# Dense values projected token-major: the input-projection weights move over stationary token rows, and the values stage is gone

## The chip, the core and the metric

One Trainium2 chip, one core of it. The metric is device time in microseconds of one execution of the whole layer, batch 1, 2048 tokens, width 1024. All times are in microseconds (us) unless marked ns. Engines: PE is the matrix engine (TensorE; its weight loads are listed apart, as PEld), DVE the vector engine, ACT the scalar engine, POOL GpSimd; SP is the engine that here only issues DMAs.

## The reference, cut to what matters

A transformer layer with two groups of attention heads that share one input projection.

```python
h = rmsnorm(x, norm1_g) * (1 + sc1) + sh1
proj = h @ w_in                                   # (2048, 3280)
aq, ak, av, bq, bk, bv, iq, ik, iw = split_columns(proj)   # av: 512 columns
for each block of 128 queries:
    # group A: differential attention, 4 heads, two softmax maps per head
    attn = softmax(q1 @ k1.T * scale + bias) - lam * softmax(q2 @ k2.T * scale + bias)
    oa = rmsnorm(attn @ av[:q_end], subln_g) * (1 - lam_init)
    # group B: an indexer scores every key, top 256 keys per query, 8 heads share bk, bv
    score = sum_h iw[:, h] * relu(iq[:, h] @ ik.T)
    ob = softmax over the chosen keys of (q @ bk.T) @ bv
x = x + g1 * (concat(oa, ob) @ w_out)
x = x + g2 * (relu(h2 @ w_ff1) ** 2 @ w_ff2)
return rmsnorm(x, final_g)
```

`av`, the dense values, are the 512 projection columns this change is about. In `attn @ av` the matrix engine needs them with tokens on the partitions.

## The kernel before

Four stages follow one another. Every projection product is made of three matmuls, since each float32 operand is split into a high and a low part (hi·hi, hi·lo, lo·hi).

**Index projection** (`index_projection`) normalises and turns x into `ht_hi` and `ht_lo`: 1024 features on partitions (8 slices `k`), four groups `g` of 512 tokens. It projects the indexer's columns.

**Indexing** (`indexing`, some 765 us) does two things at once. The indexer's scores (L825 on PE, relu on ACT at L857, weighted add on DVE at L928) and, for blocks 2 to 11, a bisection for the top 256 (counts on ACT, judging on DVE). In between, as filler on PE, the 17 remaining column tiles of the input projection (`REST_TILES`, tiles 0 to 16 of 128 columns; 8 to 11 hold the dense values and are `FULL_TILES`). A tile has four units, one for each group of 512 tokens; a unit has eight steps, one for each `k`, of three matmuls (L843: 128 weight columns loaded, 512 tokens moving). Such a unit is evacuated by ACT (L883) and, for the low part, by DVE (L988), and stored to DRAM by POOL's queue, features on rows. A unit of a full tile has no low part (ACT L879, stored at L774 to `scr.av`, features on rows too).

The order on each engine is fixed at build time by `indexing_plan`: a greedy pass over streams of jobs with assumed costs. A projection step is assumed to cost 0.68 us on PE and comes after score jobs in priority. A unit's first step waits for the evacuation of the unit four before.

**Values** (`values`): loads `scr.av` group by group, turns it on PE (four transposes for 128 tokens, L1050), copies it to `va` with ACT (L1030); and turns the sparse group's values `bv` from its two parts by a product with an identity (L1052), copied to `vb` by DVE (L1036).

**Attention** (`attention`): order again from a plan. SP loads the query units and the keys, group of 512 by group; PE makes scores (L2582), DVE reads them with the bias table added (L2795), ACT takes exponentials, PE turns the probabilities (L2598) and multiplies by `va` (L2619) or `vb` (L2613). One tile `mixst` takes a group's output, and POOL's queue stores it (L2547); the next group's output waits for that store. POOL begins with resetting semaphores, two `iota`s (L2520, L2523) from which DVE builds the bias table, and a load of one saved score block (`rank_in`, L2531). Then `output_mlp`, bound by PE, follows.

Each stage's block of instructions ends with POOL waiting for all stores; the engines meet there.

## Time and profile before

| | us |
|---|---|
| time, median of 3 runs | 3682.78 |
| lowest and highest run | 3681.52, 3685.25 |
| span of the profiled execution | 3673.6 |
| PE busy, share of the span | 88% |
| indexing: first to last projection matmul | 356.8 to 1121.9 |
| values stage: first to last matmul | 1136 to 1163 |
| attention's first score | 1168.46 |

The three runs are not listed with the profiled execution's own time apart from them; its span is 9.2 us below their median, and that is what lies around the span. In the profile a matmul's duration (0.39 us at 512 columns) is longer than the distance to the next one, because they overlap. How fast PE runs is read from the distance between starts.

### The profile page before, as it was taken

What the parts mean: (1) busy time and instruction counts of PE and PEld (TensorE: products, weight loads), DVE (VectorE), ACT (ScalarE), POOL (GpSimd) and SP (SyncE); (2) the same over time, 40 slices, a digit from 0 to 9 for tenths busy, and PEclk for the clock granted to TensorE, in tenths of its full rate; (3) what the DMA queues carried; (4) which work ended last, traced back from release to release, by engine and by line L of the source; (5) the groups of instructions that cost most, each with busy time, mean ns of one, the idle gap of its engine ahead of it and who ended that gap; (6) DMA issues with size and microseconds to landing.
All of it is one profiled execution on the core that took longest, in us unless ns stands there. A gap on an engine that the chain in (4) does not pass through costs nothing. (4 is left out here: it accounts for less than half of the span.)

```text
span 3673.6 us, 44993 instructions
## 1 busy us (share of the span) xinstructions
PE 3250.9 (88%) x15808; PEld 2610.3 (71%) x15808; DVE 2538.3 (69%) x4800; ACT 1831.4 (50%) x3051; POOL 368.9 (10%) x587
## 2 busy tenths in 40 slices
PE   4986888899797798977789989889989999999999
PEld 3775666777685576755667768768868887888887
DVE  6542688877892677676776657788887875665676
ACT  3211677877673787878867643332232222322233
POOL 1010011110101100000000000012212220000131
PEclk8997999999896899999899999989999999999999
DMA  6354333322336432111111124644454445664565
GB/s 220 126 196 121 106 105 102 95 84 67 103 101 189 127 99 65 48 45 32 39 35 30 52 101 162 218 149 155 147 171 155 155 146 206 223 235 155 199 214 206
DMA packets 334617, 475.95 MB, mean 130 GB/s; under 512 B 29056, under 2 KB 218704, under 8 KB 333984
## 3 DMA queue, kind: packets, MB, share of 16 engines
q1 hardware_dynamic: 285936, 308.29, 26.6%
q0 software_dynamic: 48464, 164.88, 12.7%
q8 instruction: 123, 2.02, 0.2%
q14 instruction: 94, 0.77, 0.1%
HBM read 316.07 MB, written 156.98 MB: 129 GB/s over the span
## 5 line engine op out<-in xcount | busy, mean ns | idle before, releaser
L2099 PE MATMUL m_ps<-m_h,w_hi 128*128 128x512 f32 x1792 | 560.7, 395 | 43.1 <-DVE m_h L1728 21.0
L2099 PEld LDWEIGHTS m_ps<-m_h,w_hi 128*128 128x128 f32 x1792 | 340.9, 191 | 117.7 <-DVE m_h L1728 30.0
L928 DVE SCALAR_TENSOR_TENSOR rank<-spare,iw,rank 128x1024 f32<-128x1024 f32 (+5 forms) x330 | 332.1, 1021 | 69.7 <-ACT spare L857 64.5
L2116 PE MATMUL m_ps<-w_hi,a_hi 128*128 128x512 f32 x896 | 350.7, 391 | 12.0 <-DVE w_lo L1936 8.9
L2099 PE MATMUL m_ps<-m_h,w_lo 128*128 128x512 f32 x896 | 352.7, 394 | 0.0
L2116 PE MATMUL m_ps<-w_lo,a_hi 128*128 128x512 f32 x896 | 350.2, 391 | 0.0
L2116 PE MATMUL m_ps<-w_hi,a_lo 128*128 128x512 f32 x896 | 350.1, 391 | 0.0
L857 ACT ACTIVATE spare<-isps 128x1024 f32<-128x1024 f32 (+5 forms) x352 | 279.7, 812 | 114.5 <-PE isps L825 80.7
L825 PE MATMUL isps<-ki,iq_hi 128*128 128x512 f32 (+3 forms) x608 | 238.8, 394 | 88.9 <-ACT spare L857 68.7
L2659 ACT ACTIVATE pt<-tps 128x512 f32<-128x512 f32 (+1 forms) x432 | 233.3, 573 | 109.6 <-PE tps L2598 53.1
L2598 PE MATMUL tps<-ident,probs 128*128 128x128 f32 x1632 | 238.7, 287 | 46.0 <-DVE probs L2814 28.7
L2598 PEld LDWEIGHTS tps<-ident,probs 128*128 128x128 f32 x1632 | 190.1, 146 | 97.8 <-DVE probs L2814 36.7
L2795 DVE CUSTOM_DVE_ANT_0 probs<-sps,bias 128x1024 f32<-128x1024 f32 (+7 forms) x176 | 165.8, 962 | 124.2 <-PE tps L2598 70.8
L2647 ACT ACTIVATE probs<-probs,stat 128x128 f32<-128x128 f32 (+15 forms) x192 | 231.1, 1204 | 34.5 <-DVE stat L2804 34.2
L864 ACT ACTIVATE below<-rank,tk 128x640 int8<-128x640 f32 (+9 forms) x210 | 228.6, 1090 | 39.1 <-DVE tk L957 35.9
L1516 ACT ACTIVATE a_hi<-a_lo 128x2048 fp32r<-128x2048 f32 x56 | 107.3, 1916 | 271.5 <-DMA a_lo<-dram_aop 271.5
L825 PE MATMUL isps<-ki,iq_lo 128*128 128x512 f32 (+3 forms) x608 | 228.7, 385 | 0.0
L843 PE MATMUL r_ps<-ht_hi,r_w_hi 128*128 128x512 f32 x544 | 219.5, 404 | 8.8 <-DVE r_ev_lo L988 5.7
L1933 DVE TENSOR_TENSOR a_lo<-a_lo,a_hi 128x2048 fp32r<-128x2048 f32 x56 | 141.2, 2521 | 117.9 <-ACT a_hi L1516 117.7
L825 PEld LDWEIGHTS isps<-ki,iq_hi 128*128 128x128 f32 x608 | 120.3, 198 | 140.5 <-ACT spare L857 54.1
L843 PE MATMUL r_ps<-ht_lo,r_w_hi 128*128 128x512 f32 x544 | 217.2, 399 | 0.0
L843 PE MATMUL r_ps<-ht_hi,r_w_lo 128*128 128x512 f32 x544 | 215.9, 397 | 0.0
(285 smaller groups left out, 7032.8 us busy)
## 6 DMA issues: line engine op xcount, KB each, us to landing
w_raw<-in_w_ff SPq DMA_DIRECT2D x136, 512.0 KB, 5.3
dram_aop<-a_out POOLq DMA_DIRECT2D x224, 256.0 KB, 2.6
a_lo<-dram_aop SPq DMA_DIRECT2D x56, 1024.0 KB, 5.3
ada_w<-in_w_ada POOLq DMA_DIRECT2D x16, 1024.0 KB, 6.6
q_hi<-dram_proj_hi SPq DMA_DIRECT2D x128, 128.0 KB, 3.0
q_lo<-dram_proj_lo SPq DMA_DIRECT2D x128, 128.0 KB, 3.0
iq_hi<-dram_proj_hi SPq DMA_DIRECT2D x224, 64.0 KB, 2.4
iq_lo<-dram_proj_lo SPq DMA_DIRECT2D x224, 64.0 KB, 2.5
```

The source lines that it names most:

```text
L825: mm = nc.tensor.matmul(sps[:, job.n % 2, a:b], q[:, job.unit % IQU, job.head % 2, :], ki[:, job.c * SCH + a:job.c * SCH + b], start=part ...
L843: mm = nc.tensor.matmul(ps[:, job.n % 4, :], a[:, i % 2, job.part, :], b[:, job.g, job.part, :], start=job.part == 0 and m == 0, stop=job. ...
L857: nc.scalar.activation(spare[:, job.n % 2, 0:job.width], sps[:, job.n % 2, 0:job.width], ACT.Relu).then_inc(s_relu, 1)
L864: nc.scalar.activation(below[:, q, 0:length].bitcast(I8), ranks[job.k % 3][:, 0:length], ACT.Sign, bias=tk[:, q, TK_NT:TK_NT + 1], accum_o ...
L928: nc.vector.scalar_tensor_tensor(out=dst, in0=got, scalar=w, in1=dst, op0=ALU.mult, op1=ALU.add).then_inc(s_acc, 1)
L1933: nc.vector.tensor_tensor(s_lo[:, c % RING], s_lo[:, c % RING].bitcast(F32), s_hi[:, c % RING].bitcast(F32), ALU.subtract).then_inc(c_sl, 1)
L2099: mm = nc.tensor.matmul(ps[:, b], w[:, m % WOPS, k, :], hop[:, j, h, :, k, :], start=fresh and k == 0 and i == 0, stop=k == KH - 1 and i == 2,
L2116: mm = nc.tensor.matmul(ps[:, t], a[:, c % RING, k, t * P:(t + 1) * P], w[:, c % RING, k, :], start=first and i == 0, stop=last and i == 2 ...
L2598: tr = nc.tensor.transpose(tps[:, job.turn % TR, (2 * kk + hh) * P:(2 * kk + hh + 1) * P], probs[:, g.heads[hh] % 4, (job.first + kk) * P: ...
L2647: nc.scalar.activation(row, row, ACT.Exp, bias=stat[:, job.hm % 8, 2:3], scale=slope, accum_out=stat[:, job.hm % 8, 3:4]).then_inc(s_exp, 1)
L2659: nc.scalar.activation(pt[:, job.slot % PT, 0:width], tps[:, job.of.turn % TR, 0:width], ACT.Copy).then_inc(s_te, 1)
L2795: nc.vector.tensor_tensor_reduce(out=row[:, job.c * SCH:job.c * SCH + job.width], in0=sps[:, job.score.n % 2, 0:job.width], in1=add, scale ...
```

## The change

1. The full tiles come last in `REST_TILES`, after all tiles that have a low part.
2. For them operands change places: the token rows `ht` are loaded as the stationary operand (128 tokens), and 128 weight columns move over them. A step has 12 matmuls of 128 columns in place of 3 of 512; a unit 96 in place of 24. The plan's assumed costs are the same as before.
3. The unit's result then has tokens on partitions; it is stored token-major, `scr.av` being `[SEQ, 512]`, 128 partitions by 4 pieces of 512 bytes.
4. `values` is gone. POOL's queue loads `va` straight from `scr.av` in four pieces of 1024 KB: the first after the two iotas, the others after the first three stores of attention outputs. PE waits for a piece where it first uses it.
5. `bv` is loaded whole in attention and turned there by 32 small matmuls between the first and the second score; DVE copies `vb` once.
6. The waits for the last stores of indexing move from the end of its block into attention's POOL stream (`last_stores`, `s_settled`). SP loads the first keys piece by piece with a semaphore each (`s_first`), query units 1 and 2 between them.

```diff
-        self.av = t("av", [A_HEADS * 2 * DH, SEQ])
+        self.av = t("av", [SEQ, A_HEADS * 2 * DH])
...
-REST_TILES = list(range(INDEX_TILES[0]))
 FULL_TILES = range(R_AV // P, R_AV // P + 4)
+REST_TILES = [tile for tile in range(INDEX_TILES[0]) if tile not in FULL_TILES] + list(FULL_TILES)
...
-                        pool.dma_start(scr.av[row:row + P, job.g * GT:(job.g + 1) * GT],
-                                       ev_hi[:, job.n % 2, :].bitcast(F32)).then_inc(s_st[job.n % 2], 16)
+                        tok = slice(job.g * GT, (job.g + 1) * GT)
+                        pool.dma_start(scr.av[tok, row:row + P].rearrange("(t p) e -> p t e", p=P),
+                                       ev_hi[:, job.n % 2, :].bitcast(F32).rearrange("p (t e) -> p t e", e=P)
+                                       ).then_inc(s_st[job.n % 2], 16)
...
-                for n in range(2):
-                    pool.wait_ge(s_st[n], 16 * stored[n])
-                    pool.wait_ge(s_mst[n], 16 * ((SPLIT - 2) // 2))
-                for n in range(3):
-                    pool.wait_ge(s_kept[n], 16 * kept[n])
+                last_stores.extend([(s_st[n], 16 * stored[n]) for n in range(2)])
...
+                        if job.tile in FULL_TILES:
+                            t = job.part * WT // KT
+                            tok = slice(t * P, (t + 1) * P)
+                            steps_of = KT * WT // KT
+                            for k in range(job.part * steps_of % KT, job.part * steps_of % KT + steps_of):
+                                for m, (a, b) in enumerate(((ht_hi, w_hi), (ht_lo, w_hi), (ht_hi, w_lo))):
+                                    mm = nc.tensor.matmul(ps[:, job.n % 4, tok], a[:, job.g, k, tok], b[:, i % 2, k, :],
+                                                          start=k == 0 and m == 0, stop=k == KT - 1 and m == 2,
+                                                          skip_group_check=True)
...
-def values(nc, keep, scr, late, block, va, vb):
...
             load_unit(0)
-            for dst, row in places:
-                load_keys(dst, row, 0)
+            for n in range(A_HEADS):
+                load_keys(*places[n], 0, s_first[n])
+            for part, src in enumerate((scr.proj_hi, scr.proj_lo)):
+                sp.dma_start(bv[:, part].bitcast(F32), src[R_BV:R_BV + DH, :]).then_inc(s_bv, 16)
+            load_unit(1)
...
+            for signal, count in last_stores:
+                pool.wait_ge(signal, count)
+            pool.sem_inc(s_settled, 1)
+
+            def load_values(g):
+                pool.dma_start(va[:, g * TG:(g + 1) * TG, :],
+                               scr.av[g * GT:(g + 1) * GT, :].rearrange("(n p) e -> p n e", p=P)).then_inc(s_va[g], 16)
+
+            load_values(0)
...
                     outs += 1
+                    if outs < NG:
+                        load_values(outs)
...
+                    if job.n == 1:
+                        pe.wait_ge(s_idv, 1)
+                        pe.wait_ge(s_bv, 32)
+                        for kt in range(NB):
+                            for part in range(2):
+                                mm = nc.tensor.matmul(sps[:, 1, kt * DH:(kt + 1) * DH],
+                                                      bv[:, part, kt * P:(kt + 1) * P], ident_r[:],
+                                                      start=part == 0, stop=part == 1)
+                        mm.then_inc(s_vt, 1)
+                        pe.wait_ge(s_vb, 1)
...
+                        if kt // TG == valued:
+                            pe.wait_ge(s_va[valued], 16)
+                            valued += 1
```

The names in the rows below: `isps` are the indexer's score sums, `r_ps` the sums of the projection tiles, `sps` attention's scores. A row says output, the moving operand, the loaded operand, and the output's shape.

PE at the end of indexing, before: the last score job, and the first of the 84 projection matmuls that follow it.

```order
L825 MATMUL isps<-ki,iq_hi 128x512
L825 MATMUL isps<-ki,iq_lo 128x512
L843 MATMUL r_ps<-ht_hi,r_w_hi 128x512
L843 MATMUL r_ps<-ht_lo,r_w_hi 128x512
L843 MATMUL r_ps<-ht_hi,r_w_lo 128x512
```

The same place in the changed kernel.

```order
L827 MATMUL isps<-ki,iq_hi 128x512
L827 MATMUL isps<-ki,iq_lo 128x512
L850 MATMUL r_ps<-r_w_hi,ht_hi 128x128
L850 MATMUL r_ps<-r_w_hi,ht_lo 128x128
L850 MATMUL r_ps<-r_w_lo,ht_hi 128x128
```

After the last score now stand 660 matmuls of 128 columns (55 steps) where 84 of 512 (28 steps) stood; 876 of 128 columns stand between scores, from score matmul 788 of 1216 on.

PE where attention begins, before.

```order
L1050 MATMUL v_psum<-ident,av_t 128x128 x4
L1052 MATMUL w_psum<-ident_v,bv_t 128x64 x2
L2559 UNCONDITIONAL_BRANCH
L2582 MATMUL sps<-ka,q_hi 128x128
L2582 MATMUL sps<-ka,q_lo 128x128
```

And in the changed kernel.

```order
L850 MATMUL r_ps<-r_w_lo,ht_hi 128x128
L739 UNCONDITIONAL_BRANCH
L2542 UNCONDITIONAL_BRANCH
L2578 MATMUL sps<-ka,q_hi 128x128
L2578 MATMUL sps<-ka,q_lo 128x128
L2562 MATMUL sps<-ident_v,bv_t 128x64 x32
L2578 MATMUL sps<-ka,q_hi 128x128
L2578 MATMUL sps<-ka,q_lo 128x128
```

The values stage's 96 instructions are gone, and 32 of them stand behind the first score. POOL's queue at the start of attention, before:

```order
L2520 IOTA second 128x2048
L2523 IOTA probs 128x128
L2531 DMA rank_in<-dram_ranks 128x1664
L2547 DMA dram_mix<-mixst 128x256 x2
L2547 DMA dram_mix<-mixst 128x128 x4
```

And in the changed kernel.

```order
L2490 IOTA second 128x2048
L2493 IOTA probs 128x128
L2500 DMA va<-dram_av 128x4x512
L2505 ISA
L2512 DMA rank_in<-dram_ranks 128x1664
L2528 DMA dram_mix<-mixst 128x256
L2500 DMA va<-dram_av 128x4x512
L2528 DMA dram_mix<-mixst 128x256
L2500 DMA va<-dram_av 128x4x512
L2528 DMA dram_mix<-mixst 128x128
L2500 DMA va<-dram_av 128x4x512
```

A load of values now stands ahead of each of the second, third and fourth output store.

## Rows read from the trace of the kernel before

**Rows 1.** The page: span, and the slices' granted clock in tenths

```profile
span 3673.6 us, 44993 instructions
...
PEclk8997999999896899999899999989999999999999
```

**Rows 2.** Busy time of the engines by stretch; then clock, DMA share, GB/s

```profile
core 0: us, PE busy (x) PEld busy (x) DVE busy (x) ACT busy (x) POOL busy (x), PEclk, DMA share, GB/s
356.00:934.00 578.00, 499.65 (x2108) 396.71 (x2109) 452.53 (x1031) 430.43 (x716) 64.66 (x110) 0.94 0.31 93
934.00:970.00 36.00, 21.60 (x95) 17.04 (x94) 31.08 (x47) 22.92 (x31) 2.70 (x5) 0.86 0.17 54
970.00:1103.00 133.00, 129.83 (x565) 104.09 (x566) 117.58 (x109) 95.72 (x106) 14.96 (x26) 0.97 0.35 114
1122.30:1169.00 46.70, 26.40 (x99) 20.01 (x99) 6.12 (x21) 12.15 (x21) 3.60 (x5) 0.55 0.80 213
```

**Rows 3.** The same stretches, projection matmuls (L843) alone: PE, PEld

```profile
356.00:934.00 578.00, 340.61 (x1320) 249.45 (x1320) 0.94 0.31 93
970.00:1103.00 133.00, 50.45 (x181) 33.68 (x182) 0.97 0.35 114
1103.00:1122.30 19.30, 19.24 (x84) 15.45 (x83) 1.00 0.36 136
```

**Rows 4.** The same stretch, score matmuls (L825) alone: PE, PEld

```profile
356.00:934.00 578.00, 208.33 (x788) 151.41 (x789) 0.94 0.31 93
```

**Rows 5.** Timeline, weight loads around two pairs of 128-column matmuls: start, duration

```profile
435.38 0.19 PEld L825 LDWEIGHTS isps<-ki,iq_lo 128*128 128x128 f32 x1
435.49 0.19 PEld L825 LDWEIGHTS isps<-ki,iq_hi 128*128 128x128 f32 x1
435.60 0.19 PEld L825 LDWEIGHTS isps<-ki,iq_lo 128*128 128x128 f32 x1
```

**Rows 6.** Timeline, the matmuls there

```profile
435.38 0.22 PE L825 MATMUL isps<-ki,iq_hi 128*128 128x128 f32 x1
435.44 0.27 PE L825 MATMUL isps<-ki,iq_lo 128*128 128x128 f32 x1
435.55 0.45 PE L825 MATMUL isps<-ki,iq_hi 128*128 128x512 f32 x1
```

**Rows 7.** Timeline, weight loads in attention, clock full, merged runs

```profile
1300.29 1.07 PEld L2598 LDWEIGHTS tps<-ident,probs 128*128 128x128 f32 x10 [0.79 <-DVE probs L2814]
...
1302.12 2.31 PEld L2619 LDWEIGHTS ops<-va,pt 128*128 128x128 f32 x20
```

**Rows 8.** Timeline, the end of indexing on ACT and POOL

```profile
1122.28 0.69 ACT L883 ACTIVATE r_ev_hi<-r_ps,r_scale 128x512 fp32r<-128x512 f32 x1 [4.80 <-PE r_ps L843]
1124.58 0.54 POOL L780 DMA_DIRECT2D dram_proj_lo<-r_ev_lo  x1
1128.85 1.83 POOL L2520 IOTA second<- 128x2048 int32 x1 [3.73 <-DMA dram_proj_lo<-r_ev_lo]
```

**Rows 9.** Timeline, SP's queue: values' first load, and attention's loads

```profile
1128.09 0.40 SPq L1021 DMA_DIRECT2D av_t<-dram_av  x1
...
1150.50 1.26 SPq L2485 DMA_DIRECT2D q_hi<-dram_proj_hi  x2
1151.80 1.27 SPq L2485 DMA_DIRECT2D q_lo<-dram_proj_lo  x2
1153.12 0.61 SPq L2494 DMA_DIRECT2D ka<-dram_proj_hi  x1
1153.78 0.60 SPq L2494 DMA_DIRECT2D ka<-dram_proj_lo  x1
```

**Rows 10.** Timeline, PE: the values stage (one of 16 rounds), the first two scores

```profile
1137.52 1.12 PE L1050 MATMUL v_psum<-ident,av_t 128*128 128x128 f32 x4
1138.57 0.63 PE L1052 MATMUL w_psum<-ident_v,bv_t 64*128 64x64 f32 x2
1139.13 1.11 PE L1050 MATMUL v_psum<-ident,av_t 128*128 128x128 f32 x4
...
1168.46 0.45 PE L2582 MATMUL sps<-ka,q_hi 128*128 128x128 f32 x1 [5.29 <-DMA kb<-dram_proj_lo]
...
1168.92 0.41 PE L2582 MATMUL sps<-ka,q_hi 128*128 128x128 f32 x1
```

**Rows 11.** DMAs from 1120 to 1200: count, KB each, median us to landing

```profile
av_t<-dram_av SPq DMA_DIRECT2D x4, 1024.0 KB, 5.7
dram_mix<-mixst POOLq DMA_DIRECT2D x4, 64.0 KB, 2.4
```

**Rows 12.** Low-part evacuations on DVE (L988): min/median/max ns

```profile
L988 DVE SCALAR_TENSOR_TENSOR r_ev_lo<-r_ps,r_scale,r_ev_hi x52: 741/746/752, 373.0 to 1123.0; 128x512 fp32r<-128x512 f32 x52
```

More of the change, by code:

```diff
@@ L1058 @@
+    return last_stores
 P_A11, P_S2, P_A12, P_S1, P_S3, P_S4, P_A22 = range(7)
@@ L2449, in attention @@
         ops = ctx.enter_context(nc.psum_tensor("ops2", [P, 2 * P], F32))
-        s_k = [sem(f"s_k_in{n}") for n in range(NG)]
+        s_first = [sem(f"s_first_k_in{n}") for n in range(2 * A_HEADS + 1)]
+        s_k = [sem(f"s_k_in{n}") for n in range(1, NG)]
+        s_va = [sem(f"s_va_in{n}") for n in range(NG)]
+        s_bv = sem("s_bv_in")
+        s_idv = sem("s_ident_v")
+        s_settled = sem("s_last_stores_over")
+        s_vt = sem("s_bv_turned")
+        s_vb = sem("s_vb")
         s_q = [sem(f"s_q_in{n}") for n in range(QU)]
@@ L2494, in load_keys @@
                     sp.dma_start(dst[r * DH:(r + 1) * DH, keys].bitcast(F32),
-                                 src[row:row + DH, keys]).then_inc(s_k[g], 16)
+                                 src[row:row + DH, keys]).then_inc(signal, 16)
             def load_chosen(b):
@@ L2499, in load_chosen @@
                     sp.wait_ge(s_bias, b - 2)
+                if b == 3:
+                    sp.wait_ge(s_settled, 1)
                 sp.dma_start(chosen[:, 0:P * (b + 1)], scr.masks[b, :, 0:P * (b + 1)]).then_inc(s_ch, 16)
             load_unit(0)
-            for dst, row in places:
-                load_keys(dst, row, 0)
+            for n in range(A_HEADS):
[3 more added lines that the diff above has]
+            load_unit(1)
+            for n in range(A_HEADS, 2 * A_HEADS):
+                load_keys(*places[n], 0, s_first[n])
+            load_unit(2)
+            load_keys(*places[-1], 0, s_first[-1])
             load_chosen(2)
-            pieces = [(dst, row, g) for g in range(1, NG) for dst, row in places]
-            for n in range(1, len(units)):
+            pieces = [(dst, row, g, s_k[g - 1]) for g in range(1, NG) for dst, row in places]
+            for n in range(QU, len(units)):
                 load_unit(n)
-                if n <= len(pieces):
-                    load_keys(*pieces[n - 1])
+                if n - QU < len(pieces):
+                    load_keys(*pieces[n - QU])
                 b = units[n][1]
@@ L2574, in _ @@
                         pe.wait_ge(s_sf, before.read)
+                    if job.n == 1:
[8 more added lines that the diff above has]
+                        pe.wait_ge(s_vb, 1)
+                    place = 2 * A_HEADS if job.what == "sparse" else 2 * job.head + (job.what == "map2")
+                    if place not in first_places:
+                        first_places.add(place)
+                        pe.wait_ge(s_first[place], 32)
                     keys = kb if job.what == "sparse" else ka[:, 2 * job.head + (job.what == "map2"), :]
@@ L2638, in _ @@
         def _(act):
+            nc.scalar.activation(ident_r[:], keep.ident[0:DH, 0:DH], ACT.Copy).then_inc(s_idv, 1)
             for half in range(2):
@@ L2864, in hybrid_block @@
                 vb = inner.enter_context(nc.sbuf_tensor("vb", [P, NB, DH], F32))
-                s_va, s_vb = values(nc, keep, scr, late, block, va, vb)
-                done = attention(nc, keep, scr, late, block, va, vb, s_va, s_vb, spent)
+                done = attention(nc, keep, scr, late, block, va, vb, last_stores, spent)
             output_mlp(nc, keep, scr, late, block, done, x, subln_g, w_out, w_ff1, w_ff2, final_g, out)
```

102 lines of the change are left out of this document (31 added, 71 removed).

## The prediction

> **What bounds the kernel now.** I went from the page to the stretches, and from there to the single instructions. The page says that PE is what nearly the whole span is made of, at a clock mostly full [rows 1], so a change that adds PE work has to find idle PE time or cost its length. The table of stretches cuts the part that is touched. From 356 to 934 indexing has PE 86% busy and DVE 78%, neither full [rows 2]: scores, relus and adds wait for one another. From 970 to 1103 PE is 98% busy [rows 2]. From 1103 to 1122.3 there is nothing left but 84 projection matmuls in 19.3 us, with PE full [rows 3]: 0.229 us each, which is the distance between two of 512 columns at the full clock (2.4 GHz). I take 0.228. Then comes a stretch of 46.7 us in which PE has 26.4 us of small work at a clock of 0.55 [rows 2]: the meeting of the engines, the values stage, the first loads of attention.
>
> So in the first half the touched work hides partly, in the second half not at all.
>
> **The change part by part.**
>
> *The price of one 128-column matmul with its own load.* The trace before has this very shape: scores of 640 keys end in a hi and a lo matmul of 128 columns. The first to second start is 0.06 us apart, what 128 columns take; but the second to the next is 0.11 [rows 6], because the loads stand 0.11 apart, 435.38, 435.49, 435.60 [rows 5]. A 512-column matmul hides such a load, a 128-column one does not: the stream runs at the pace of the loads. Long runs at full clock say the same: 10 loads in 1.07 us, 0.107 each, and 20 in 2.31, 0.1155 or less each [rows 7]. I take 0.11, with 0.107 and 0.115 as ends.
>
> The 16 full units have 384 matmuls at 0.228, 87.6 us, before, and 1536 at 0.11, 169.0 us, after: **81.4 us more PE work** in the indexing stage for the same product. The evacuations (ACT 0.6 to 0.7 us each) and stores are as many as before and have ten microseconds a unit; they are hidden. The token-major stores have more and shorter pieces, and also have that time.
>
> The Trainium skill, "TensorE: Matmul & The Clock Gate", section "Back-to-back issue gap", gives 81 ns for a stream of loads and 128-column matmuls, and 131 ns at 512 columns. The rows above contradict the second (0.229) and stand above the first (0.11). By its 81 ns the 1536 would take 124 us, 37 more than before; the sum below does not use it.
>
> *Where it stands.* The plan that fixes the order still assumes 0.68 us for a step, and a step is now 12 × 0.11 = 1.32 us. And by moving tiles with a low part forward it delays steps behind DVE's evacuations, so fewer steps find a place between scores: 55 steps (660 matmuls) stand behind the last score where 28 (84) stood. I add up in three pieces, counting in the order and pricing scores at 0.228 (512 columns), 0.168 (384) and 0.114 (256, 128).
>
> (a) Up to score matmul 788, at 934 us in the trace [rows 4]. Before, 1320 projection matmuls stand ahead of it [rows 3]; after, 1248: 72 fewer, 16.4 us less PE work. But 52 units with a low part are done by then in place of 39 (1320/24 = 55 units less the 16 full), 13 × 0.746 us [rows 12] = 9.7 us more on DVE. With both engines waiting for each other in this stretch I take 0, with ends −16 (PE decides) and +10 (DVE decides).
>
> (b) From score 788 to 1216, 934 to 1103 us, 169 us. Before: 228 projection matmuls 52.0 + 428 score matmuls 90.6 = 142.6 of PE work, so 26 us of real gaps, some 16 of them before 970 (PE busy 21.6 of 36 there [rows 2]). After: 90.6 + 876 × 0.11 = 96.4, together 187.0. The added 44 us fill gaps first: I leave 7 of the 16 and 4 of the other 10, since more filler ahead of a score makes PE the one that is waited for. 187 + 11 = 198, **+29**. Ends: no gap left, +18; all gaps left, +44.
>
> (c) Behind the last score: 660 × 0.11 = 72.6 against 19.3, **+53**. Nothing else is there to hide it: DVE and ACT have no work left but evacuations. Ends 51 (at 0.107) and 57 (at 0.115).
>
> Indexing: 0 + 29 + 53 = **+82**.
>
> *The values stage.* Count from ACT's last evacuation, 1122.28 [rows 8]. Before, the second score begins at 1168.92 [rows 10], 46.6 later: both stores to land (SP goes on at 1128.09 [rows 9]), then 1 MB and 16 rounds of 1.61 us on a cold PE [rows 10], then keys and queries, of which the first score waits for the last one (5.29 us, kb [rows 10]). After: ACT 0.7, POOL's issue by +1.9, SP begins at about +2.1, since nobody waits for landing. Four query loads take 2.6 us of its queue, eight key loads 0.64 each, 5.1 [rows 9]; the two loads of bv 1.2: issued at +11. They are 512 KB each; with a landing somewhat under the 5.7 us of 1 MB [rows 11], +16. The 32 matmuls: a round of 1.61 less the four transposes' 1.12 is 0.49 for two [rows 10], 16 × 0.49 = 7.8 us cold (3.5 if the clock were full): +24. DVE's copy of 1024 columns some 1 us: the second score at +25. Gain 46.6 − 25 = **−22**. POOL's iotas (2.1 us, from +2) and DVE's table stood beside the values stage and are now in front of the first read, but end by +6, before the first score can be there (+9): nothing. Ends: −30 (fast landing, warm clock) and −14 (DMA slow while the queue is full).
>
> *Attention's start.* The loads of the pieces 1 to 3 of va (1 MB, 5.7 us [rows 11]) each go onto POOL's queue ahead of an output store that takes 2.4 us alone [rows 11], and the single `mixst` makes the next group wait for it. Groups come every 4 to 5 us there, so a store meets only the last microseconds of a load: 1 to 2 us three times, +4 (ends 0 and 12). Queries of units 1 and 2 come earlier, −1. **+3**. The rest of attention and the MLP have the same order and move as a whole.
>
> Sum: 82 − 22 + 3 = +63. Against the median, since the 9 us around the span stay: 3682.8 + 63 = **3746 us**, slower by 1.7%.
>
> **The rivals.**
>
> *The column pace decides (not slower).* If in a long row of these matmuls the loads ran under the matmuls completely, one would cost 0.057, half of 0.114 for 256 columns. Then (a) gives up to −8, (b) 876 × 0.057 = 50 against 52, −2, (c) 38 against 19, +18; with −22 and +3 it is −11: **3672**. For it speaks only that first distance of 0.06 [rows 6]; against it the loads' own distances [rows 5, 7]. It decides where the pace falls under about 0.066.
>
> *Halfway.* If the load is half hidden, 0.083 each: (c) 54.8, +35.5; (b) 90.6 + 72.7 = 163 with 14 us of gaps, +8; (a) 0; with −19: **3707**. The Trainium skill's 81 ns of that section ("TensorE: Matmul & The Clock Gate", "Back-to-back issue gap") is this case.
>
> *The gaps take it.* The stage has 119 us of gaps before 934. If the earlier placing lets PE run ahead, (a) is −16 and (b) +18: 55 − 22 + 3: **3719**. Against it: those gaps are waits for DVE and ACT, and the order is fixed.
>
> *Starved scores.* Each step ahead of a score now delays relu and add by 0.6 us more; where DVE, at 88% from 970 to 1103 [rows 2], then misses its turn, gaps add to gaps: (a) +10, (b) +44, (c) +57, less 19: **3775**, up to 3790.
>
> *The handover does not get shorter.* bv's load, 32 cold matmuls and the copy in a row, plus va's loads on the queue: gain 8 in place of 19: **3757**.
>
> **How the numbers follow.** Forecast 60% (its own range 3725 to 3770), column pace 6%, halfway 8%, gaps 10%, starved 9%, handover 7%. The likeliest is 3746. The range 3705 to 3785 takes in all but the column pace and the far end of starvation. A measurement can tell 0.2%, 7.4 us, from no change. Faster is the column pace alone, 6%; within 0.2% the space between it and halfway, 3%; slower the rest, 91%.
>
> **What would show it.** The 128-column matmuls at 0.107 to 0.115 us from start to start, loads at the same distance; the first of them 930 to 940 us into the span; the last score near 1132; 73 us of nothing but L850 behind it, and indexing's last matmul near 1204; the second score 25 us later, in place of 47; attention and MLP as long as before. I am wrong if L850's starts stand under 0.09 apart, if the last score comes before 1115 or after 1150, or if the first blocks of attention wait for va or for stores by more than 12 us.

## The result, and the profile after

The changed kernel takes 3759.07 us in the median of 4 runs (3751.91 to 3761.83), the kernel before on the same chip 3682.15 us (4 runs, 3676.18 to 3685.25). The ratio is 1.0202, with a 95% interval from 1.0186 to 1.0217: 76.9 us slower. The forecast was 3746, its range 3705 to 3785.

The profiled execution of the changed kernel has a span of 3750.0 us against 3673.6 [rows 1], so 76.4 us more: the two executions show nearly the whole difference of the medians. The changed kernel's profiled execution took 3751.91 us, so 1.9 us lie around its span and not the 9.2 named ahead of the prediction; it is 7 us under its median, and by the same 1.9 us so is that of the kernel before (an estimate, 3675.5), so the difference between the two stays. The page's span, and the granted clock in tenths, slice by slice:

```profile
span 3750.0 us, 47131 instructions
...
PEclk9997999989999699998889999989999999999999
```

The clock is as full as it was; time went somewhere else. The same stretches as in [rows 2], cut at the same events (score matmul 788, the last score, ACT's last evacuation, the second attention score). The columns are busy time and count of PE, PEld, DVE, ACT and POOL, then clock, DMA share and GB/s:

```profile
356.00:933.40 577.40, 488.37 (x2035) 386.09 (x2035) 461.80 (x1053) 434.01 (x718) 71.45 (x123) 0.92 0.32 98
933.40:1133.20 199.80, 193.77 (x1306) 177.06 (x1305) 140.21 (x137) 113.67 (x131) 13.57 (x20) 0.98 0.24 75
1133.20:1207.10 73.90, 73.90 (x662) 73.81 (x660) 2.04 (x2) 4.62 (x7) 5.06 (x7) 1.00 0.11 37
1207.10:1239.30 32.20, 7.76 (x36) 7.40 (x35) 3.54 (x8) 3.03 (x7) 4.13 (x5) 0.55 0.91 224
```

The first stretch is as long as before, the second has grown from 169 to 199.8 us and the third from 19.3 to 73.9. In the third the clock is full and PE never idle. The fourth has shrunk. Of the projection in token order alone (L850), PE, PEld, clock, DMA share, GB/s:

```profile
933.40:1133.20 199.80, 104.11 (x876) 104.82 (x877) 0.98 0.24 75
1133.20:1207.10 73.90, 73.71 (x660) 73.81 (x660) 1.00 0.11 37
```

660 of them stand behind the last score, and 73.9 us for 660 is **0.112 us each**. In that stretch the weight loads are as busy as the matmuls: 73.81 of 73.9 us. The timeline at 1150 us, first the matmuls and then the weight loads, start and duration:

```profile
1150.08 0.27 PE L850 MATMUL r_ps<-r_w_hi,ht_hi 128*128 128x128 f32 x1
1150.19 0.28 PE L850 MATMUL r_ps<-r_w_hi,ht_lo 128*128 128x128 f32 x1
1150.31 0.28 PE L850 MATMUL r_ps<-r_w_lo,ht_hi 128*128 128x128 f32 x1
```

```profile
1150.14 0.19 PEld L850 LDWEIGHTS r_ps<-r_w_hi,ht_lo 128*128 128x128 f32 x1
1150.25 0.19 PEld L850 LDWEIGHTS r_ps<-r_w_lo,ht_hi 128*128 128x128 f32 x1
1150.36 0.19 PEld L850 LDWEIGHTS r_ps<-r_w_hi,ht_hi 128*128 128x128 f32 x1
```

Matmuls and loads both stand 0.11 apart. This is the distance that the pair of short matmuls in the kernel before had shown [rows 5, 6].

The handover, on PE (the brackets give the idle time ahead and what ended it), and on SP's queue:

```profile
1215.12 0.44 PE L2578 MATMUL sps<-ka,q_hi 128*128 128x128 f32 x1 [7.92 <-DMA ka<-dram_proj_lo]
1230.97 7.01 PE L2562 MATMUL sps<-ident_v,bv_t 64*128 64x64 f32 x32 [15.20 <-DMA bv_t<-dram_proj_lo]
1239.30 0.47 PE L2578 MATMUL sps<-ka,q_hi 128*128 128x128 f32 x1 [1.32 <-DVE vb L2783]
```

```profile
1216.43 0.61 SPq L2471 DMA_DIRECT2D bv_t<-dram_proj_hi  x1
1217.09 0.60 SPq L2471 DMA_DIRECT2D bv_t<-dram_proj_lo  x1
```

ACT's last evacuation starts at 1207.23 and the second score at 1239.30, 32.1 us later, where it was 46.6 [rows 8, 10]. Of these 32, PE sits 15.2 waiting for `bv_t`, issued at 1216.4 and 1217.1 and there at 1230.97.

### The profile page after: what moved, and what is told of

It is laid out like the page before. It is cut to its first block and busy times, and to the rows that moved or that the text cites. A ratio compares the mean times of both kernels' runs of the same rounds, so it can differ in the third digit from the quotient of the medians.

```text
span 3750.0 us, 47131 instructions
## 1 busy us (share of the span) xinstructions
PE 3317.9 (88%) x16896; PEld 2700.3 (72%) x16896; DVE 2533.5 (68%) x4785; ACT 1822.4 (49%) x3035; POOL 378.4 (10%) x591
## 5 line engine op out<-in xcount | busy, mean ns | idle before, releaser
L2066 PEld LDWEIGHTS m_ps<-w_hi,a_hi 128*128 128x128 f32 x896 | 169.2, 189 | 48.8 <-issue 9.3
L1442 ACT ACTIVATE w_hi<-w_raw 128x512 fp32r<-128x512 f32 x128 | 80.1, 626 | 249.2 <-DVE w_raw L1711 249.2
L1353 POOL DMA_DIRECT2D dram_aop<-a_out x224 | 121.4, 542 | 769.8 <-DVE a_out L1815 389.3
```

The lines of the kernel that those rows point to most:

```text
L1353: pool.dma_start(scr.aop[op, row:row + P, half * GT:(half + 1) * GT], act_in[:, op, :]).then_inc(q_a[op], 16)
L2066: mm = nc.tensor.matmul(ps[:, t], a[:, c % RING, k, t * P:(t + 1) * P], w[:, c % RING, k, :], start=first and i == 0, stop=last and i == 2 ...
```

## The experiments

All times below are medians; "before" is the kernel before on the same chip. Where milestones are given they are of the profiled execution of each kernel, one trace each. Indexing runs from the first projection matmul to the last; the handover from ACT's last evacuation to the second attention score; attention from there to the first matmul of the output projection.

| kernel | last score | indexing | handover | attention | span | median | ratio, 95% |
|---|---|---|---|---|---|---|---|
| before | 1102.6 | 765.1 | 46.6 | 993.8 | 3673.6 | 3682.15 | |
| after | 1133.2 | 851.3 | 32.1 | 999.7 | 3750.0 | 3759.07 | 1.0202 [1.0186, 1.0217] |
| wstat | 1100.5 | 782.5 | 34.2 | 1002.1 | 3685.8 | 3687.15 | 1.0006 [0.9996, 1.0016] |
| order_only | 1101.5 | 779.3 | 44.3 | 999.3 | 3694.3 | 3693.35 | 1.0023 [1.0014, 1.0033] |
| pair256 | 1103.2 | 799.4 | 33.0 | 1001.1 | 3711.3 | 3705.54 | 1.0052 [1.0036, 1.0069] |
| pair_spread | 1109.8 | 773.5 | 32.0 | 1001.6 | 3681.2 | 3682.25 | 1.0003 [0.9992, 1.0013] |
| plan_cost | 1129.6 | 861.7 | 32.7 | 1002.9 | 3763.5 | 3765.97 | 1.0222 [1.0201, 1.0243] |
| bv_first | 1137.3 | 851.1 | 21.2 | 1001.8 | 3745.5 | 3749.88 | 1.0192 [1.0172, 1.0211] |
| va_later | 1137.4 | 855.9 | 32.5 | 998.4 | 3753.6 | 3756.20 | 1.0205 [1.0188, 1.0221] |
| best1 | 1101.6 | 775.5 | 21.3 | 1005.1 | 3665.5 | 3671.94 | 0.9974 [0.9965, 0.9983] |

From execution to execution the first projection matmul itself starts anywhere from 352 to 363 us, which is why lengths are compared and not ends. Lengths of the same code differ too: the indexing of after, bv_first and va_later is one and the same, with 851.3, 851.1 and 855.9 us; attention is the same in before and order_only, with 993.8 and 999.3. A difference of 5 us between two traces is therefore not a finding by itself. The stretch behind attention is 1510.8 to 1511.3 us in all but one of these (pair256 1514.1).

### Half the columns: is it the load?

If a short matmul costs what its weight load costs, moving 64 columns in place of 128 saves nothing. Against the changed kernel:

```diff
-  matmul(ps[:, job.n % 4, tok], a[:, job.g, k, tok], b[:, i % 2, k, :], ...
+  matmul(ps[:, job.n % 4, t * P:t * P + DH], a[:, job.g, k, tok],
+         b[:, i % 2, k, 0:DH], ...
```

> The changed kernel with 64 of each tile's 128 weight columns moving over the token rows; the loads stay. Half of the dense values' products is left out, the rest of the program is the same. Load pace decides (my theory): starts of L850 stay 0.11 us apart, 74 us behind the last score, the time stays at 3750 to 3762 us. Column pace decides: starts 0.055 apart, 37 us behind the last score, about 3675 us.

It took 3845.47 us in its one execution (before: 3683.98), 86 us more than the kernel with twice the columns. Neither theory had that. While scores still stand between the projections, the weight loads are 0.11 apart, with half the columns as with all of them, so the load theory's first statement holds:

```profile
1149.88 0.19 PEld L850 LDWEIGHTS r_ps<-r_w_hi,ht_lo 128*128 128x128 f32 x1
1149.99 0.19 PEld L850 LDWEIGHTS r_ps<-r_w_lo,ht_hi 128*128 128x128 f32 x1
...
1160.27 0.33 PEld L850 LDWEIGHTS r_ps<-r_w_lo,ht_hi 128*128 128x128 f32 x1
1160.48 0.33 PEld L850 LDWEIGHTS r_ps<-r_w_hi,ht_hi 128*128 128x128 f32 x1
```

Ten microseconds later they are 0.21 apart. The stretches (PE, PEld, DVE, ACT, POOL, clock, DMA share, GB/s) say why; the first row is from the beginning of these matmuls:

```profile
950.00:960.00 10.00, 10.00 (x43) 9.42 (x42) 1.66 (x3) 3.19 (x5) 0.00 (x0) 0.50 0.00 0
...
1150.00:1160.00 10.00, 10.00 (x80) 9.51 (x78) 6.25 (x5) 4.67 (x6) 1.30 (x2) 1.00 0.19 66
...
1170.00:1180.00 10.00, 10.00 (x49) 10.00 (x48) 0.00 (x0) 0.00 (x0) 0.74 (x1) 0.50 0.10 28
```

The last score is at 1155.1. Behind it, with nothing but L850 left, the granted clock goes to 0.50, the 1.2 GHz level, though PE had been issuing without a pause and stays 100% busy. Over the 110 us from 1170 on one matmul costs 0.213 us, where the changed kernel does 0.112 in the same place at clock 1.00: the distance doubles as the clock halves. From the last score to the last projection it is 136.4 us in place of 73.7. The first row shows the same thing earlier: from 945 to 989, where only a few scores stand between the projections, the clock is at 0.50 too, with PE 100% busy from 940 to 980. The changed kernel has in that place:

```profile
950.00:960.00 10.00, 10.00 (x81) 9.58 (x80) 9.72 (x13) 3.83 (x5) 0.00 (x0) 1.00 0.01 2
```

The stretch from the first projection to the last score is 15.2 us longer than the changed kernel's (792.8 against 777.6). Together this says that the price is the load's and not the columns', and that something about the clock had escaped me; two more runs follow it below.

The Trainium skill, "TensorE: Matmul & The Clock Gate", section "LDWEIGHTS (loading the stationary operand)", puts a load at its columns divided by 1.2, in ns: 107 for 128 columns. The loads' distances at full clock agree (0.11 here), those at half clock do not.

### The same kernel with weights held, tokens moving

Everything of the change but the swap of operands (the dense values land in the wrong places of `dram_av`, so the output's dense part is not the reference's):

```diff
-                        if job.tile in FULL_TILES:
-                            t = job.part * WT // KT
...
-                        else:
-                            for m, (a, b) in enumerate(((w_hi, ht_hi), (w_hi, ht_lo), (w_lo, ht_hi))):
...
+                        for m, (a, b) in enumerate(((w_hi, ht_hi), (w_hi, ht_lo), (w_lo, ht_hi))):
+                            mm = nc.tensor.matmul(ps[:, job.n % 4, :], a[:, i % 2, job.part, :],
```

> The changed kernel with the operands of the full tiles back in their old places: 128 weight columns loaded, 512 tokens moving, 3 matmuls a step. Order of the steps, token-major stores, attention's start all as changed; the dense values come out in the wrong places, that part of the computation is changed. My theory (the 1152 more loads are the whole loss in indexing): PE work 620 us, 37.6 us behind the last score in place of 74, indexing's last matmul at 1127 (1122 before, 1207 changed), time 3679 us. Rival (stores, order or start of attention carry a good part of the loss): above 3700 us.

3687.15 us (10 runs, 3681.00 to 3691.57), 8 us more than I had expected, and as fast as the kernel before within what can be told. So **the swap of operands is the slowdown**: 3759 less 3687 is 72 us, and between the traces the indexing stage differs by 851.3 − 782.5 = 68.8 us. The swap adds 81.4 us of PE work by the prediction's count (and 0.112 measured each); some 12 of them found idle time.

I had expected the last projection matmul at 1127, and it came at 1138. The projection matmuls of this kernel (L845) by stretch, PE, PEld, clock, DMA share, GB/s:

```profile
356.00:934.00 578.00, 323.60 (x1237) 234.51 (x1238) 0.92 0.32 97
934.00:1101.50 167.50, 63.80 (x235) 42.63 (x234) 0.96 0.30 92
1101.50:1138.90 37.40, 37.16 (x163) 30.16 (x161) 1.00 0.21 71
```

Against [rows 3] this is 1237 for 1320 up to 934 us, and 163 for 84 behind the last score, which comes only 1 us earlier (744.7 us behind the first projection, for 745.8). 79 more at 0.229 are 18 us, what this kernel's indexing is longer by (17.4). By the counts they come from the order.

### The order alone

The kernel before, with the full tiles last, as the change has them, and the column of the scales looked up by tile:

```diff
-REST_TILES = list(range(INDEX_TILES[0]))
+REST_TILES = [tile for tile in range(INDEX_TILES[0]) if tile not in FULL_TILES] + list(FULL_TILES)
-                                                     scale=scale[:, job.n // 4:job.n // 4 + 1])
+                                                     scale=scale[:, job.tile:job.tile + 1])
```

> The kernel before with one part of the change, the full tiles last (and the scales picked by tile). My theory: 55 steps behind the last score in place of 28, 37.6 us in place of 19.2, but 16 us less work ahead of score 788; last matmul of indexing near 1127, time 3687 us. Rival (the order by itself is free, since the gaps move too): 3682 us. Rival (delayed steps leave PE idle early, all 18 us are lost): 3700 us.

3693.35 us, +9.4 on the median; indexing is 14.2 us longer in the trace. That is between my 3687 and the 3700 of the rival that loses all 18. The projections of this kernel (L843):

```profile
356.00:934.00 578.00, 322.28 (x1233) 234.55 (x1234) 0.91 0.32 97
934.00:1101.50 167.50, 64.19 (x236) 42.57 (x235) 0.96 0.29 92
1101.50:1138.90 37.40, 37.22 (x163) 30.71 (x164) 1.00 0.18 71
```

The counts are those of the kernel with weights held, to a few matmuls. So the order costs 14 to 17 us of indexing in these two traces, whatever the shape: tiles with a low part, which need DVE, pulled forward leave 87 projection matmuls fewer (1320 less 1233) up to 934 us, in a stretch that is no shorter for it; they are done at the end, where nothing else is. The granted clock of that stretch is 0.91 and 0.92 for 0.94 in [rows 3]; whether the order brings this with it, one trace of the kernel before can't say. The medians give the order less: 9.4 us in all with 2.3 us won in the handover, some 12 of indexing by that (an estimate). The trace of the kernel before is 7 us under its median, that of order_only (3696.05) 2.7 over its own, which is most of what the traces differ by more than the medians.

### Two weight tiles side by side: 256 columns per load

If the load is the price, a load that serves 256 columns should be nearly free. The kernel after, with weight tiles of a pair in the two slots and moved together; there are 768 matmuls in place of 1536. The pairs stand last, as 9, 8, 11, 10, the plan frees both slots of a pair together, and the stores are regrouped to match:

```diff
-                            t = job.part * WT // KT
-                            tok = slice(t * P, (t + 1) * P)
+                            t = job.part * 2 // KT
+                            row = (job.g % 2 * 2 + t) * P
...
-  matmul(ps[:, job.n % 4, tok], a[:, job.g, k, tok], b[:, i % 2, k, :], ...
+  matmul(ps[:, job.n % 4, t * 2 * P:(t + 1) * 2 * P],
+         a[:, job.g // 2, k, row:row + P], b[:, :, k, :], ...
```

> The changed kernel with two weight tiles moving together over the same stationary token rows: 256 columns for each load, 768 matmuls in place of 1536, same product. Load pace theory: a 256-column matmul takes 0.114 us and hides its load, so the full tiles cost 87.6 us again, 47.9 us behind the last score, last matmul near 1130, time 3682 us (3675 to 3690). Rival (a stationary operand taken from the token rows, or a moving operand in two pieces, is slow by itself): 0.14 us or more each, 3705 us or more.

Their pace is as hoped. The timeline, three in a row:

```profile
1159.83 0.28 PE L868 MATMUL r_ps<-r_w_hi,ht_hi 128*128 128x256 f32 x1
...
1160.05 0.28 PE L868 MATMUL r_ps<-r_w_lo,ht_hi 128*128 128x256 f32 x1
```

Two distances in 0.22 us: 0.11 each for twice the columns. But the kernel took 3705.54 us, 22 more than before. The waits from 1100 to 1163 (us in total, times, longest):

```profile
PEld r_ps L868 <- DVE r_w_lo L1016: 10.2, 1, 10.2
PE r_ps L868 <- DVE r_w_lo L1016: 10.0, 1, 10.0
...
ACT r_w_hi L905 <- DMA r_w_raw<-in_w_in: 6.0, 1, 6.0
ACT r_w_hi L905 <- PE r_ps L868: 3.3, 1, 3.3
```

A pair occupies both weight slots. The next pair's weights are split only when the last matmul of the pair is through, and the second tile's raw weights are still to come from DRAM (6.0 us). Behind the last score no other matmul covers this, and PE stands once for 10.0 us, from 1107.8 to 1117.8; the first row is the same wait, counted on the weight loads. So the wait is 10 of the 34 us by which indexing is longer than before. Another 10 are work behind the last score: 420 of the 768 matmuls, 47.9 us at 0.114, where 165 of 512 columns (37.6 us) stand with weights held. The 14 that these leave are the size of what the order cost above; they were not taken apart. The theory of the price held; its edit brought a new wait, which I had not counted.

### The same, with tiles that need one slot between the pairs

```diff
-REST_TILES = [tile for tile in range(INDEX_TILES[0]) if tile not in FULL_TILES] + list(FULL_TILES)
+REST_TILES = [0, 1, 2, 3, 4, 5, 6, 7, 12, 13, 14, 15, 8, 9, 16, 11, 10]
```

(That line is against the changed kernel; from the kernel with both pairs last, nothing but the order differs.) The 20 us in the text below are the 10.0 us above, counted once on the matmuls and once on their loads.

> Two weight tiles move together (256 columns for each load), and the tile order is 0 to 7, 12 to 15, the pair 8 and 9, 16, the pair 10 and 11. With both pairs last PE stood 20 us waiting for weights, since a pair holds both weight slots; here one other tile stands between them. My theory: PE work 620 us, 25.3 us behind the last score, waits for weights under 6 us, last projection matmul near 1135, time 3684 us (3677 to 3691). Rival (waits for weights are as long as before): 3705 us.

3682.25 us, ratio 1.0003. The waits of L868 are gone:

```profile
  issue: 0.4, 1
  DVE r_ev_lo L1020: 0.2, 1
```

222 matmuls behind the last score take 26.3 us, 0.118 each, where half a 512-column matmul is 0.114. So with 256 columns to a load the swap of operands is free within what can be told, and the whole change comes out even: indexing +8.4 us (773.5 against 765.1), the handover −14.6, attention +7.8. It is the counter-test to the result: the same product in token order, 77 us faster than with 128 columns. Two things differ from the changed kernel, the pairs and the order of the tiles; with weights held and the changed kernel's order indexing was 782.5, so the new order accounts for some 9 of the 77.

### A plan that knows the price

The list that fixes the order still reckons 0.68 us for a step that now takes 1.34.

```diff
-                mm = put("mm", Step("mm", "PE", 0.68, where + k / 40, ...
+                mm = put("mm", Step("mm", "PE", 1.32 if full else 0.68, where + k / 40, ...
```

> The changed kernel, with the plan told that a step of a full tile takes 1.32 us in place of 0.68; it then puts 65 steps (87 us) behind the last score in place of 55, and fewer between scores. My theory (PE is full from the first full tile on, only the amount of work counts): last score 13 us earlier, last projection matmul within 5 us of the changed kernel's, time 3752 to 3765 us. Rival (the wrong cost starves DVE and costs length): 3740 us or less.

3765.97 us, just above what I expected and no gain. Telling the plan the truth makes it place fewer steps between scores: 65 steps, 780 matmuls, stand behind the last score in place of 660, and the last projection is 861.7 us behind the first, not 851.3. I had expected the last score 13 us earlier; it comes 3 us earlier, 774.6 us behind the first projection for 777.6, though 120 matmuls (13 us) were taken out from between the scores. PE is busy only 4.7 us less there (677.8 for 682.5) and idle about as long (96.8 for 95.1); the clock is 0.92 for 0.94. So PE was not full there, and the amount of work alone does not give the time. The wrong number in the plan was not part of the slowdown.

### The handover: who waits for bv

The two loads of `bv_t` go ahead of the key loads:

```diff
+            for part, src in enumerate((scr.proj_hi, scr.proj_lo)):
+                sp.dma_start(bv[:, part].bitcast(F32), src[R_BV:R_BV + DH, :]).then_inc(s_bv, 16)
...
-            for part, src in enumerate((scr.proj_hi, scr.proj_lo)):
-                sp.dma_start(bv[:, part].bitcast(F32), src[R_BV:R_BV + DH, :]).then_inc(s_bv, 16)
```

> The changed kernel with the two loads of bv put ahead of all others in SP's queue at the start of attention. In the changed kernel they are issued at 1216.4 and land at 1230.9, and the second score begins 32.1 us after ACT's last evacuation. My theory (their place in the queue and the full DMA rings are why they are late): they land by 8 us after the evacuation, the second score begins at 19 to 21, time 3747 us. Rival (the rings are full whatever the order, and the first query and key loads come later instead): second score at 29 to 32, 3757 to 3759 us.

```profile
1223.67 0.45 PE L2578 MATMUL sps<-ka,q_hi 128*128 128x128 f32 x1 [12.32 <-DMA ka<-dram_proj_lo]
1224.26 7.03 PE L2562 MATMUL sps<-ident_v,bv_t 64*128 64x64 f32 x32
1232.61 0.47 PE L2578 MATMUL sps<-ka,q_hi 128*128 128x128 f32 x1 [1.32 <-DVE vb L2783]
```

PE no longer waits for `bv_t`: the two loads land in 5.5 and 7.2 us, for 12.1 and 13.8. The keys now come later, and the first score waits 12.3 us for them in place of 7.9. ACT's last evacuation is at 1211.39, so the second score is 21.2 us behind it, 10.9 less than after. Some of this is passed on: the first output store comes 11.0 us behind the second score in place of 8.3. Attention is 2.1 us longer, and the intervals of the two ratios (1.0192 and 1.0202) overlap: the gain is plain in the trace, and by the medians (3749.88 against 3759.07) likely but not shown by itself.

### Attention's start: values' pieces against the stores

The three later pieces of `va` are issued behind output stores 8, 12 and 16, not 1, 2 and 3:

```diff
-                    if outs < NG:
-                        load_values(outs)
+                    if outs in (8, 12, 16):
+                        load_values(outs // 4 - 1)
```

> The changed kernel with the loads of pieces 1 to 3 of va behind the 8th, 12th and 16th output store in place of the 1st, 2nd and 3rd. My theory (in the first groups an output store waits in the queue behind 1 MB, and the next group waits for the store): the first six stores come 4 to 5 us faster, from second score to the first output-projection matmul 994 us as before in place of 999.7, time 3754 us. Rival (the 6 us come from the clock, or from other loads): 999.7 stays, 3759 us. Rival (the loads hurt as much where they now stand): the same.

The stores with their releasers; first of the changed kernel (store 1 and store 6), then of this one:

```profile
1247.59 0.56 POOL L2528 DMA_DIRECT2D dram_mix<-mixst  x1 [32.77 <-ACT mixst L2674]
...
1275.81 0.54 POOL L2528 DMA_DIRECT2D dram_mix<-mixst  x1 [3.09 <-ACT mixst L2684]
```

```profile
1252.18 0.56 POOL L2528 DMA_DIRECT2D dram_mix<-mixst  x1 [33.45 <-ACT mixst L2674]
...
1273.10 0.54 POOL L2528 DMA_DIRECT2D dram_mix<-mixst  x1 [2.97 <-ACT mixst L2684]
```

The six stores take 28.2 us with the pieces between them and 20.9 without (21.2 in the kernel before). So there is a delay of 7 us at the start, larger than my +3. But at the end of attention only 1.3 us of it are gained (999.7 against 998.4, medians 3759.07 and 3756.20, intervals overlapping). Where the rest stays, the stores behind the moved pieces show:

```profile
1287.45 0.76 POOL L2500 DMA_DIRECT2D va<-dram_av  x1
...
1298.94 0.54 POOL L2528 DMA_DIRECT2D dram_mix<-mixst  x1 [7.86 <-ACT mixst L2684]
```

That store, the tenth, comes 8.4 us behind the ninth, where it was 3.6 in the changed kernel and 4.0 in the kernel before. Counted from the second score, in the kernel before, the changed kernel and this one:

| output store | before | after | va_later |
|---|---|---|---|
| 7th | 37.3 | 44.2 | 37.0 |
| 13th | 66.3 | 72.5 | 70.9 |
| 25th | 130.1 | 135.4 | 136.3 |
| last (96th) | 984.9 | 990.8 | 989.6 |

The changed kernel loses 7 us by the seventh store and is still 6 behind at the last. The moved pieces lose nearly as much behind stores 8, 12 and 16. That is the second rival of the text above: the loads hurt as much where they now stand.

### All together

Pairs spread, `bv_t` first, pieces of `va` later.

> All three together: pairs of weight tiles in that order, bv's loads first, va's later pieces behind stores 8, 12 and 16. If the parts add up: 3684 less 12 less 5, 3667 us, 0.4% under the kernel before. If bv's place is worth nothing: 3679 us. If the gain in handover is eaten by attention's first blocks: 3684 us.

3671.94 us (11 runs, 3667.49 to 3677.48), 0.9974 of before with an interval from 0.9965 to 0.9983: 9.8 us faster than before, 87 faster than the changed kernel. The handover:

```profile
1128.00:1150.00 22.00, 8.27 (x39) 7.91 (x37) 3.54 (x8) 3.03 (x7) 4.09 (x5) 0.61 0.95 237
```

DMA is 95% busy and PE has 8 of 22 us: transfers are what is left there. Of the expected 3667 it misses 5 us; indexing +10.4, handover −25.3, and attention +11.3, the longest of all kernels.

### The clock with short matmuls

96 of 128 columns, and the 64 again:

```diff
-  matmul(ps[:, job.n % 4, tok], a[:, job.g, k, tok], b[:, i % 2, k, :], ...
+  matmul(ps[:, job.n % 4, t * P:t * P + 96], a[:, job.g, k, tok],
+         b[:, i % 2, k, 0:96], ...
```

> As the run with 64 columns, with 96 of each tile's 128 weight columns moving (a quarter of the dense values' products is left out). In the run with 64 the load pace held (starts as far apart as the loads), but the granted clock fell to half behind the last score, though PE never paused; with 128 it stayed full. Theory (fewer moving columns for each load, at the same pace of loads, let the clock go): with 96 either starts 0.11 apart and full clock, 74 us behind the last score and 3750 to 3762 us in all, or the half clock again and above 3800 us; I expect the first. Rival (the half clock with 64 was one bad execution): full clock here and in the repetition with 64.

> The run with 64 of 128 weight columns again (half of the dense values' products left out), same program. If the half clock belongs to the program: 3835 to 3855 us and a clock near 0.5 to 0.6 behind the last score. If it was one bad execution: 3750 to 3762 us.

3833.22 and 3841.57 us, one execution each (before: 3683.13). The half clock repeats, and 96 columns have it too. Stretches with 96 columns:

```profile
1120.00:1150.00 30.00, 30.00 (x196) 26.91 (x194) 22.29 (x20) 19.47 (x22) 1.50 (x2) 1.00 0.14 40
...
1170.00:1280.00 110.00, 110.00 (x518) 110.00 (x517) 0.00 (x0) 2.98 (x5) 3.75 (x5) 0.50 0.04 13
```

and with 64:

```profile
1170.00:1280.00 110.00, 110.00 (x517) 110.00 (x517) 0.00 (x0) 2.98 (x5) 4.50 (x6) 0.50 0.05 15
```

In both 0.213 us each, the loads busy for 100% of the time, over 110 us. With the same instructions, the same loads and 128 columns the clock is 1.00 for 73.9 us. My guess for 96 columns, that they would keep the full clock, fell. Between 1001 and the last score, where scores take about half of PE's time, the clock is 1.00 in all three runs (the first row here, and 1150 to 1160 in the 64-column table above). Where the projections first begin, with few scores among them, it falls in all three, from 945 to 989 with 64 columns and from 943 to 981 with 96; with 128 it is at its lower level only for two short times there, at 965 and 979, behind a gap of 3.5 us on PE that ends at 964.

## Why the prediction was right, and where it was off

**The price of one matmul**, the ground of the whole sum, was 0.11 (0.107 to 0.115), and 0.112 was measured. That the loads set it, and not the columns, is shown from both sides: 64 columns have the same pace at full clock, and 256 too (0.11). The column pace and the halfway rival are out. No run loads fewer than 128 columns, so whether 0.11 is a matter of the load's length or the price of any load is not shown. The halfway case was the 81 ns in the Trainium skill, "TensorE: Matmul & The Clock Gate", "Back-to-back issue gap"; this kernel shows 0.112.

**(a) Up to score 788**: 0, and it is 933.4 for 934. 72 projection matmuls fewer did not make it shorter: PE is busy 11.3 us less (488.4 for 499.7) and idle 10.7 us more, so PE doesn't decide there, which also tells against the rival of the gaps. That rival's 119 us of gaps, like the 26 us in (b), were the length less the priced work; by [rows 2] PE is idle for 78.3 and 17.6 of them, and the rest is time at the lower clock, for which the prediction has no term. With the clock at 0.92 for 0.94 here, a small gain and a small loss may have met in this 0.

**(b) 788 to the last score**: 29 forecast, 199.8 − 169 = 30.8 measured. PE is busy for 193.8 of 199.8, so 6 us of gaps are left, where I had left 11; in return PE's work there came to 193.8 for my 187.0: the 876 matmuls of L850 are busy 104.1 us, 0.119 each, where I had priced 96.4. Busy time also holds the end of each group's last matmul, which the pace does not.

**(c) Behind the last score**: 53 forecast, 73.9 − 19.3 = 54.6 measured; 660 matmuls, as counted. Indexing as a whole: +82 forecast, 84.9 between ACT's last evacuations (1207.23 less 1122.28), 86.2 from first to last matmul. The two runs that part it give the order 14 to 17 of it (some 12 by the medians), the swap 69 to 72. My sum did not name the order as a cost, but it was in the counts that it used: 1248 for 1320 in (a) at no gain in time, and 55 steps for 28 in (c).

**The handover** is the term that was mis-sized: −22 forecast, 32.1 − 46.6 = −14.5 measured, just inside its end of −14. The step that failed is "with a landing somewhat under the 5.7 us of 1 MB". I had +16 for it. Issued at +9.2 and +9.9 us, earlier than my +11, the two loads took 12.1 and 13.8 us to land, at +23.7. From 1207 to 1290, DMAs with count, KB each and median us to landing:

```profile
va<-dram_av POOLq DMA_DIRECT2D x4, 1024.0 KB, 9.4
...
bv_t<-dram_proj_hi SPq DMA_DIRECT2D x1, 512.0 KB, 12.1
bv_t<-dram_proj_lo SPq DMA_DIRECT2D x1, 512.0 KB, 13.8
```

The 5.7 us of [rows 11] were those of a megabyte in the values stage; here a dozen loads on SP's queue, and a megabyte of `va` and 832 KB of `rank_in` on POOL's, stand in front, and DMA is 91% busy. The 32 matmuls took 7.0 for 7.8, the copy 1.3. Put ahead of the keys, the same loads land in 5.5 and 7.2 us, PE does not wait for them, and the handover is 21.2: the wait was an order of transfers and not a size.

**Attention's start**: +3 forecast, +5.9 measured (993.8 to 999.7). At the start the mechanism is there, at twice the size: the third and fourth stores come 7.8 and 7.7 us behind the ones ahead, where the kernel before has 5.1 and 3.9, and the first six take 28.2 us for 21.2 (bv_first 28.0, wstat 29.7, order_only 21.0). What is left of it at the end of attention can't be told from the scatter of this stretch: the order alone, with attention's code as before, has 999.3. Attention as a whole, in the kernel before and with the order alone (PE, PEld, DVE, ACT, POOL, clock, DMA share, GB/s):

```profile
1168.92:2162.70 993.78, 848.59 (x5352) 654.48 (x5352) 681.05 (x1825) 752.59 (x1380) 57.70 (x107) 0.93 0.21 63
```

```profile
1183.86:2183.20 999.34, 852.74 (x5351) 656.74 (x5351) 680.82 (x1825) 752.74 (x1380) 57.69 (x107) 0.92 0.21 63
```

Work and order are the same; the granted clock is not. The trace of the kernel before has the least time at the lower level in attention (147 us), order_only 156, after 160, and best1 the most (172, a clock of 0.91), with 993.8, 999.3, 999.7 and 1005.1 us. So a part of these lengths goes with the clock, and how much of the +5.9 is the loads' stays open between 0 and 6.

Sum: 85 − 14.5 + 6 = 76.4 for 63. Of the 13 us that were missing, 7.5 are the handover's, 3 indexing's, 3 attention's, the last within the scatter of the traces. The measured time lies inside the forecast's own 3725 to 3770, and its two large terms, (b) and (c), came out by their mechanism; the 0 of (a) may be luck in part. **Starved scores** (3775) is the rival nearest to the number, but not what happened: its gaps did not come, PE is 97% busy from 933 to 1133.

## What to carry to other kernels

Which operand is held costs nothing in products and much in loads: each load of 128 columns needs some 256 moving columns to disappear behind, so before swapping operands look for a second tile that can move over the same stationary rows, and then for what holds its buffers. Work that has lost its cover costs its full length: count what stands behind the last instruction of the stage that hid it, since there a reordering that "moves nothing" cost some 12 to 17 us. And when a barrier goes and its loads start together, put the transfer with the longest tail of work behind it first: the same 512 KB landed in 12 to 14 us behind the others and in 5.5 to 7 ahead of them. A transfer that costs its neighbours time, as the pieces of `va` do, may cost as much wherever it is moved.

## What the runs showed of the hardware that I had not expected

- **The granted clock fell under a PE that never paused.** With 64 and with 96 moving columns to a 128-column load, PE and the loads 100% busy, the clock went from 1.00 to 0.50 within 7 us of the last score, when nothing but these matmuls was left, and stayed there to their end, 1287 to 1292 (0.213 us a matmul). With 128 columns, and the rest alike, it stayed at 1.00. With 64 columns this cost 63 us behind the last score, and most of the 15 us ahead of it goes with the earlier fall at 945; the kernel took 86 us more in all. Moving less data took more time. What makes the clock fall was not found; three executions of two kernels show that it does.
- **Load pace follows the clock**: 0.112 at full, 0.213 at half, for the same 128-column load.
- **A load of 512 KB took 12.1 and 13.8 us** among others, where a megabyte had taken 5.7.
- **What stays open**: why the traces differ in the clock granted in attention (0.91 to 0.93) and with it in its length (993.8 to 1005.1), and how much of the order's 12 to 17 us another order of the same tiles would give back; one that mixes pairs and single tiles still has +8.4.
